# Weight loads in 8 KB runs per partition, with strided columns in the transposes and the gather that match them

## The chip, the core and the metric

The kernel runs on one core of one Trainium2 chip. TensorE (PE) multiplies, and loads its stationary operand with a separate instruction (PEld) that can overlap the product before it. VectorE (DVE), ScalarE (ACT) and GpSimd (POOL) do the element work, SyncE (SP) issues every transfer, and 16 DMA engines carry them out. The metric is the device time of one execution in microseconds, the median of three runs. A program without any change in it varies by about 1% from run to run here.

## The reference

Sequence length 256, model width 1024, float32. A first block of two layers is followed by a second block with a mixture of experts. Only two parts are touched, the feed-forward part of each layer and the experts:

```
# both layers of the first block; w_down has 2816 rows
gate, up = jnp.split(h @ ffn_w_gate_up, 2, axis=-1)
x = x + g_f * ((jax.nn.silu(gate) * up) @ ffn_w_down)
...
# second block: 16 experts, w_gate and w_up 1024 x 512, w_down 512 x 1024
for e in range(N_EXPERTS):
    h = jax.nn.silu(jnp.einsum("bsd,df->bsf", x, w_gate[e])) * jnp.einsum("bsd,df->bsf", x, w_up[e])
    y = y + combine[..., e:e + 1] * jnp.einsum("bsf,fd->bsd", h, w_down[e])
```

The router gives each token two experts out of one group of four, so that each expert has to be applied only to the tokens of its group.

## The kernel before

Every weight comes through a ring. A unit is 1 MB: 128 partitions of 2048 floats (`UNIT`). SP issues a unit's transfer as soon as a raw slot is free (`Ring.feed`, L159; it waits for DVE's `lo_done`). ACT then rounds the unit to a high part (`Ring.hi`, L172), DVE subtracts to get the low part (`Ring.lo`, L184), and each product on TensorE is done three times (high by high, high by low, low by high) on single-pass operands. The layers' ring (`layer_raw`, `layer_split`) has 4 raw slots and 3 pairs, the experts' ring (`expert_raw`, `expert_split`) has 5 and 4. The units' order is fixed when the program is built, and so is the order of each engine's work.

**Feed-forward part** (`FeedForward`, 11 blocks of 256 hidden columns in each of two layers). For a block, TensorE makes gate and up products (L459, 96 matmuls with 256 moving columns), the previous block's down product (L1894, 24 matmuls with 512 moving columns) and four transposes of the gated hidden values (L1882), whose results ACT and DVE split into `ffnh_aT` (L1929, L1962). The down weights of a block are one unit: 256 rows of 1024 floats. Partition p holds rows p and 128 + p of the block, so the transposes take hidden columns 0 to 127 and 128 to 255, each a run of neighbouring columns. In layer 0 the ring also brings the modulation weights `ada_w`, which DVE sums (L199 to L208).

**Experts** (`routed_experts`). After the routing, 16 pairs of gather matmuls (L2448, 32 in all) put the tokens of the four groups side by side: the stationary operand is a 128 x 128 piece of `x_pair`, columns 128c to 128c + 127, and the result is chunk c of the transposed tokens. Each expert then is 48 matmuls for gate and up (L2399, two units each), four transposes of the hidden values (L2410) and 24 matmuls for down (L2423, two units). In a gate or up unit partition p holds rows 128(k0 + k) + p for four k, so four runs of 512 floats; in a down unit two runs of 1024 floats.

In a transpose the stationary operand is the tile that is turned, and the moving one is the identity matrix, so the columns picked out by the slice in the code are the ones that the weight load reads.

Of the kernel before, what the change touches and what calls it, by code (L numbers as in the profile page):

```python
# [20 lines left out]
P = 128  # L21
D = 1024
S = 256
TILES = S // P
KD = D // P
# [7 lines left out]
D_EXPERT = 512  # L33
ALPHA = 2 ** 0.25
UNIT = 8 * 256
# [190 lines left out]
def program(nc, A, OUT):  # L226
    es = ExitStack()
    with es:
# [3 lines left out]
        ps = [es.enter_context(nc.psum_tensor(f"bank{b}", [P, 512], FP)) for b in range(8)]  # L232
# [14 lines left out]
        ident, ones = const("ident"), const("ones")  # L247
# [522 lines left out]
        def layers():  # L770
# [6 lines left out]
            def add(unit):  # L777
                units.append(unit)
                return len(units) - 1
# [21 lines left out]
            def layer_units(l, beside_proj, beside_gates, beside_ffn):  # L801
                w = {"proj": [], "gates": [], "branch": [], "out": []}
                p = pending_ada(beside_proj)
                w["proj"] = [None] * 8
                for i in (2, 3, 0, 1, 4, 5, 6, 7):
                    w["proj"][i] = add_cols("w_in", l, 256 * i, min(256 * i + 256, 1952))
                    ada_next(p)
                p = pending_ada(beside_gates)
                for b in range(12):
                    w["gates"].append(add_cols("w_in", l, 1952 + 256 * b, 2208 + 256 * b))  # L810
                    if b >= 7:
                        ada_next(p)
                for nb in range(2):
                    n0, n1 = 512 * nb, 512 * nb + 512

                    def part(name, row, k):
                        return (row * 512, k, 512, 0, 512, cols(name, l, n0, n1))

                    w["branch"].append((add([part("w_br_na", 0, 2), part("w_br_mla", 2, 2)]),
                                        add([part("w_br_gqa", 0, 4)])))  # L820
                for nb in range(4):
                    w["out"].append(add_cols("w_out", l, 256 * nb, 256 * nb + 256))
                p = pending_ada(beside_ffn)
                many = len(beside_ffn) > 1
                w["gu"], w["dn"] = [], []

                def down(n):
                    w["dn"].append(add([(0, 2, D, 0, D, A["ffn_w_down"][l, 256 * n:256 * n + 256, :]
                                         .rearrange("(k p) n -> p k n", p=P))]))
                    if many and n in (2, 4, 6, 8):  # L830
                        ada_next(p)

                for n in range(n_hidden):
                    pair = []
                    for up in range(2):
                        c0 = FFN * up + 256 * n
                        pair.append(add_cols("ffn_w_gate_up", l, c0, c0 + 256))
                        if many and n or (up and n in (1, 3, 5, 7)):
                            ada_next(p)
                    w["gu"].append(pair)  # L840
                    if n:
                        down(n - 1)
                down(n_hidden - 1)
                return w

            p = pending_ada([(0, 0), (0, 1)])
# [5 lines left out]
            with ExitStack() as st:  # L852
# [51 lines left out]
                for l in range(DEPTH):  # L904
                    LAYER[0] = f"_{l}"
                    w = where[l]
# [926 lines left out]
        class FeedForward:  # L1833
# [26 lines left out]
            def tensor(self, pe):  # L1860
                ring, ada, blocks, norm, gu, dn = self.ring, self.ada, self.blocks, self.norm, self.gu, self.dn

                def hidden(n, up, t):
                    ring.arrived(pe, gu(n, up))
                    if n >= 1 and t == 0:
                        pe.wait_ge(self.acted if up else self.multiplied, n)
                    job, out = Job(gu(n, up), "tok", t, 256, True, None), ps[up][:, t * 256:(t + 1) * 256]
                    if n:
                        ins = products(ring, job, out)
                    else:  # L1870
                        products(ring, job, out, pe, norm.ready(t), chunks=norm.ORDER[0:4], last=False)
                        if up and t == 0:
                            norm.turn(pe, 1)
                        ins = products(ring, job, out, pe, norm.ready(t), chunks=norm.ORDER[4:8], first=False)
                    if t == 1:
                        ins.then_inc(ring.used, 1)

                def turn(n):
                    pe.wait_ge(self.acted, n + 1)
                    for t in range(TILES):  # L1880
                        for c in range(2):
                            ins = nc.tensor.transpose(ps[2][:, c * S + t * P:c * S + (t + 1) * P],  # L1882
                                                      self.a[:, t, c * P:(c + 1) * P], ident)
                    ins.then_inc(self.turned, 1)

                def down(n):
                    pe.wait_ge(self.lo_out, n + 1)
                    ring.arrived(pe, dn(n))
                    for t in range(TILES):
                        for nb in range(2):  # L1890
                            for c in range(2):
                                for tp, wp in ((0, 0), (0, 1), (1, 0)):
                                    w = ring.view(dn(n), wp, 2, D)
                                    ins = nc.tensor.matmul(  # L1894
                                        ps[4 + 2 * t + nb][:, :], self.aT[:, tp, c, t * P:(t + 1) * P],
                                        w[:, c, nb * 512:(nb + 1) * 512],
                                        start=n == 0 and c + tp + wp == 0,
                                        stop=n == blocks - 1 and c == 1 and tp == 1)
                        if n == blocks - 1 and t == 0:
                            ins.then_inc(self.tile_sum, 1)  # L1900
                    ins.then_inc(ring.used, 1)

                for n in range(blocks):
                    for up, t in ((0, 0), (1, 0), (0, 1), (1, 1)) if n == 0 else ((0, 0), (0, 1), (1, 0), (1, 1)):
                        hidden(n, up, t)
                    if n and ada.due(gu(n, 0)):
                        ada.reduce(pe, 3, 1)
                        self.reduced_in[n] = 1
                    if n >= 1:
                        down(n - 1)  # L1910
                    turn(n)
                down(blocks - 1)
                self.ada_end = ada.done_pe
# [24 lines left out]
            def add(self, dve, t, half):  # L1938
                cut = slice(512 * half, 512 * half + 512)
                done(dve, nc.vector.tensor_tensor(self.buf.tmp[half], ps[4 + 2 * t + half][:, :], self.gate[:, cut], ALU.mult),  # L1940
                     self.step)
                done(dve, nc.vector.tensor_tensor(x[:, t, cut], x[:, t, cut], self.buf.tmp[half], ALU.add), self.added)
# [105 lines left out]
        def second_part():  # L2048
# [34 lines left out]
                return A[name][0, e, :, 256 * n:256 * n + 256].rearrange("(k p) n -> p k n", p=P)  # L2083

            expert_units, dense_units = [], []
            def rows_of(name, e, k0, k):
                return A[name][0, e, P * k0:P * (k0 + k), :].rearrange("(k p) n -> p k n", p=P)

            for e in range(N_EXPERTS + 1):
                if e < N_EXPERTS:  # L2090
                    for name in ("w_gate_2", "w_up_2"):
                        expert_units += [[(0, 4, 512, 0, 512, rows_of(name, e, k0, 4))] for k0 in (0, 4)]
                if e:
                    expert_units += [[(0, 2, D, 0, D, rows_of("w_down_2", e - 1, k0, 2))] for k0 in (0, 2)]
            n_hidden = N_EXPERTS * D_EXPERT // 256
            per = D_EXPERT // 256
            dense_units = hidden_units(n_hidden, lambda n: expert_half("w_gate_2", n // per, n % per),
# [20 lines left out]
            with ExitStack() as st:  # L2118
# [7 lines left out]
                with ExitStack() as s1:  # L2126
                    xP = sb("x3_pair", [P, 2, TILES, D], s1, FR)
# [220 lines left out]
        def routed_experts(ring, comb, xP, G, st, scratch, route, g_ready, combined):  # L2348
# [34 lines left out]
            with nc.Block() as block:  # L2383
# [9 lines left out]
                def _(pe):  # L2393
# [11 lines left out]
                    def turn(e):  # L2405
                        pe.wait_ge(acted, e + 1)
                        if e >= 1:
                            pe.wait_ge(a_lo, e)
                        for c in range(4):
                            ins = nc.tensor.transpose(ps[TURN][:, c * P:(c + 1) * P], act_[:, c * P:(c + 1) * P], ident)  # L2410
                        ins.then_inc(turned, 1)

                    def down(e):
# [29 lines left out]
                    for n in range(16):  # L2443
# [1 line left out]
                        if n >= 7:  # L2445
                            pe.wait_ge(*left(n - 7))
                        for t in range(TILES):
                            ins = nc.tensor.matmul(ps[PICK[n % 7]][:, :], xP[:, part, t, c * P:(c + 1) * P],  # L2448
                                                   G[:, t, :, :].rearrange("p g s -> p (g s)"), start=t == 0, stop=t == 1)
                        ins.then_inc(picked, 1)  # L2450
                        if n in TABLES:
# [1116 lines left out]
```

## Time and profile before

| | us |
|---|---|
| median of 3 runs | 1805.93 |
| lowest, highest run | 1790.78, 1807.78 |
| span of the profiled execution | 1795.4 |
| TensorE busy in it | 1597.9 (89%) |
| VectorE busy | 1225.5 (68%) |
| ScalarE busy | 817.2 (46%) |
| granted TensorE clock, mean share of full | 0.950 |

The span runs from the first to the last instruction of the profiled execution, which is another execution than the three timed ones. Matmuls are pipelined: the recorded time of one is longer than the distance from its start to the next one's. So a stretch of matmuls is best read by the starts of its groups.

### The profile page before, as it was taken

What the parts mean: (1) busy time and instruction counts of PE and PEld (TensorE: products, weight loads), DVE (VectorE), ACT (ScalarE), POOL (GpSimd) and SP (SyncE); (2) the same over time, 40 slices, a digit from 0 to 9 for tenths busy, and PEclk for the clock granted to TensorE, in tenths of its full rate; (3) what the DMA queues carried; (4) which work ended last, traced back from release to release, by engine and by line L of the source; (5) the groups of instructions that cost most, each with busy time, mean ns of one, the idle gap of its engine ahead of it and who ended that gap; (6) DMA issues with size and microseconds to landing.
All of it is one profiled execution on the core that took longest, in us unless ns stands there. A gap on an engine that the chain in (4) does not pass through costs nothing. (4 is left out here: it accounts for less than half of the span.)

```text
span 1795.4 us, 25499 instructions
## 1 busy us (share of the span) xinstructions
PE 1597.9 (89%) x10701; PEld 1443.7 (80%) x10701; DVE 1225.5 (68%) x1352; ACT 817.2 (46%) x945; POOL 43.9 (2%) x60
## 2 busy tenths in 40 slices
PE   2899998999899999899969998886788969999995
PEld 2789987999788988899959898775687767888884
DVE  4877586888757648656554885533565868889895
ACT  1345543433334554434323564224443337777773
POOL 0100000000010000000000000000000000000000
PEclk9989999999999999999989999987787989999998
DMA  8974435999844324566436463111231637999992
GB/s 306 316 236 141 163 121 172 351 331 325 276 139 145 110 94 164 182 215 230 137 110 197 147 188 118 47 48 31 64 118 34 203 138 262 370 343 369 357 357 100
DMA packets 226057, 348.07 MB, mean 194 GB/s; under 512 B 14612, under 2 KB 156672, under 8 KB 225808
## 3 DMA queue, kind: packets, MB, share of 16 engines
q1 hardware_dynamic: 225936, 346.36, 57.7%
q8 instruction: 87, 1.43, 0.3%
q14 instruction: 34, 0.28, 0.0%
HBM read 345.29 MB, written 1.97 MB: 193 GB/s over the span
## 5 line engine op out<-in xcount | busy, mean ns | idle before, releaser
L459 PE MATMUL bank<-layer_split,hT_pair 128*128 128x256 f32 (+2 forms) x4032 | 514.3, 288 | 29.7 <-DVE hT_pair L1031 21.0
L459 PEld LDWEIGHTS bank<-layer_split,hT_pair 128*128 128x128 f32 x4032 | 488.0, 191 | 43.6 <-issue 28.9
L184 DVE TENSOR_TENSOR layer_split<-layer_raw,layer_split 128x2048 fp32r<-128x2048 f32 x122 | 279.6, 2292 | 101.6 <-ACT layer_split L172 99.9
L172 ACT ACTIVATE layer_split<-layer_raw 128x2048 fp32r<-128x2048 f32 x122 | 233.6, 1915 | 192.0 <-PE bank L459 76.9
L184 DVE TENSOR_TENSOR expert_split<-expert_raw,expert_split 128x2048 fp32r<-128x2048 f32 x96 | 219.1, 2289 | 30.4 <-ACT expert_split L172 30.2
L172 ACT ACTIVATE expert_split<-expert_raw 128x2048 fp32r<-128x2048 f32 x96 | 183.6, 1917 | 59.0 <-PE bank L2399 32.8
L459 PE MATMUL bank<-split_w,hT_pair 128*128 128x256 f32 (+1 forms) x1248 | 173.2, 301 | 14.9 <-PEq L2600 5.0
L459 PEld LDWEIGHTS bank<-split_w,hT_pair 128*128 128x128 f32 x1248 | 163.1, 201 | 25.7 <-issue 17.1
L184 DVE TENSOR_TENSOR split_w<-raw_w,split_w 128x2048 fp32r<-128x2048 f32 x52 | 119.2, 2292 | 64.2 <-ACT split_w L172 63.6
L1894 PE MATMUL bank<-layer_split,ffnh_aT 128*128 128x512 f32 x528 | 127.0, 396 | 2.8 <-DVE ffnh_aT L1962 2.8
L172 ACT ACTIVATE split_w<-raw_w 128x2048 fp32r<-128x2048 f32 x52 | 99.4, 1912 | 58.9 <-PE bank L459 50.1
L459 PE MATMUL bank<-hT_pair,split_w 128*128 128x256 f32 x960 | 119.5, 285 | 5.5 <-DVE hT_pair L315 4.8
L459 PEld LDWEIGHTS bank<-hT_pair,split_w 128*128 128x128 f32 x960 | 116.9, 192 | 7.4 <-issue 5.7
L1894 PEld LDWEIGHTS bank<-layer_split,ffnh_aT 128*128 128x128 f32 x528 | 98.0, 188 | 25.8 <-DVE ffnh_aT L1962 3.3
L2423 PE MATMUL bank<-expert_split,expert_hidden_T 128*128 128x512 f32 x384 | 92.3, 396 | 1.4 <-DVE expert_hidden_T L2563 1.4
L2399 PE MATMUL bank<-expert_split,hT_pair 128*128 128x512 f32 x384 | 92.5, 397 | 0.9 <-ACT gathered_pair L2492 0.9
L2399 PE MATMUL bank<-expert_split,gathered_pair 128*128 128x512 f32 x384 | 90.8, 392 | 0.0
L2423 PEld LDWEIGHTS bank<-expert_split,expert_hidden_T 128*128 128x128 f32 x384 | 72.1, 188 | 18.9 <-DVE expert_hidden_T L2563 1.6
L2399 PEld LDWEIGHTS bank<-expert_split,hT_pair 128*128 128x128 f32 x384 | 71.5, 188 | 18.0 <-ACT gathered_pair L2492 1.3
L2399 PEld LDWEIGHTS bank<-expert_split,gathered_pair 128*128 128x128 f32 x384 | 71.5, 188 | 14.9
L204 DVE SCALAR_TENSOR_TENSOR ada_acc<-layer_raw,silu_c,ada_acc 128x1024 f32<-128x1024 f32 x40 | 51.7, 1294 | 1.4
L1929 ACT ACTIVATE ffnh_aT<-bank 128x512 fp32r<-128x512 f32 x22 | 13.1, 597 | 80.0 <-PE bank L1882 80.0
(459 smaller groups left out, 1795.1 us busy)
## 6 DMA issues: line engine op xcount, KB each, us to landing
layer_raw<-in_ada_w SPq DMA_DIRECT2D x48, 1024.0 KB, 6.7
layer_raw<-in_ffn_w_gate_up SPq DMA_DIRECT2D x44, 1024.0 KB, 5.6
raw_w<-in_w_in SPq DMA_DIRECT2D x40, 1024.0 KB, 5.4
layer_raw<-in_w_in SPq DMA_DIRECT2D x38, 1024.0 KB, 5.9
expert_raw<-in_w_gate SPq DMA_DIRECT2D x32, 1024.0 KB, 7.5
expert_raw<-in_w_up SPq DMA_DIRECT2D x32, 1024.0 KB, 7.4
expert_raw<-in_w_down SPq DMA_DIRECT2D x32, 1024.0 KB, 7.1
layer_raw<-in_ffn_w_down SPq DMA_DIRECT2D x22, 1024.0 KB, 5.1
```

The source lines that it names most:

```text
L172: self.nc.scalar.activation(self.pair[:, j % self.pairs, 0, 0:self.size[n]], self.raw[:, n % self.depth, 0:self.size[n]], ACT.Copy).then_i ...
L184: self.nc.vector.tensor_tensor(self.pair[:, j % self.pairs, 1, 0:self.size[n]], self.raw[:, n % self.depth, 0:self.size[n]], self.pair[:, ...
L204: self.nc.vector.scalar_tensor_tensor(acc[:, :], second, self.scale[:, 2 * q + 1:2 * q + 2], acc[:, :], ALU.mult, ALU.add).then_inc(self.l ...
L459: ins = nc.tensor.matmul(out, lhs, rhs, start=first and c == chunks[0] and tp + wp == 0, stop=last and c == chunks[-1] and tp == 1)
L1894: ins = nc.tensor.matmul(ps[4 + 2 * t + nb][:, :], self.aT[:, tp, c, t * P:(t + 1) * P], w[:, c, nb * 512:(nb + 1) * 512], start=n == 0 an ...
L1929: nc.scalar.activation(self.aT[:, 0, :, :].rearrange(flat), ps[2][:, :], ACT.Copy).then_inc(self.hi_out, 1)
L2399: ins = nc.tensor.matmul(ps[bank][:, :], gathered[e // PER // 2][:, tp, 4 * i + c, slot_cut(e // PER)], ring.view(u + i, wp, 4, 512)[:, c, :],
L2423: ins = nc.tensor.matmul(ps[OUT_BANKS[nb]][:, :], aT[:, tp, 2 * i + c, :], ring.view(u + i, wp, 2, D)[:, c, nb * 512:(nb + 1) * 512], star ...
```

## The change

The same weights go into the same units in the same order, but in each unit a partition now holds neighbouring rows of the matrix. A gate or up matrix of an expert is read as 128 partitions of 8 neighbouring rows, 16 KB each, and the two units are the first and the second 8 KB of each partition; a down matrix is 128 partitions of 4 neighbouring rows, again 16 KB in two halves; a block of `ffn_w_down` is 128 partitions of 2 neighbouring rows, 8 KB. The transfer's source is then one run of 2048 floats for each partition.

The contraction index that sits on partition p, chunk k, becomes K p + k rather than 128 k + p, with K = 2, 8 and 4. To match, the feed-forward transposes take every second column, the gather takes every eighth column of `x_pair`, and the experts' transposes take every fourth column of the hidden values. The products themselves, and the number and the order of the instructions on every engine, stay as they were.

```
--- before.py
+++ after.py
                 def down(n):
-                    w["dn"].append(add([(0, 2, D, 0, D, A["ffn_w_down"][l, 256 * n:256 * n + 256, :]
-                                         .rearrange("(k p) n -> p k n", p=P))]))
+                    w["dn"].append(add([(0, 1, UNIT, 0, UNIT, A["ffn_w_down"][l, 256 * n:256 * n + 256, :]
+                                         .rearrange("(p k) n -> p (k n)", p=P).unsqueeze(1))]))
...
                             ins = nc.tensor.transpose(ps[2][:, c * S + t * P:c * S + (t + 1) * P],
-                                                      self.a[:, t, c * P:(c + 1) * P], ident)
+                                                      self.a[:, t, c:256:2], ident)
...
-            def rows_of(name, e, k0, k):
-                return A[name][0, e, P * k0:P * (k0 + k), :].rearrange("(k p) n -> p k n", p=P)
+            def run_of(name, e, i):
+
+                return A[name][0, e, :, :].rearrange("(p k) n -> p (k n)", p=P)[:, UNIT * i:UNIT * (i + 1)].unsqueeze(1)
...
-                        expert_units += [[(0, 4, 512, 0, 512, rows_of(name, e, k0, 4))] for k0 in (0, 4)]
+                        expert_units += [[(0, 1, UNIT, 0, UNIT, run_of(name, e, i))] for i in range(2)]
                 if e:
-                    expert_units += [[(0, 2, D, 0, D, rows_of("w_down_2", e - 1, k0, 2))] for k0 in (0, 2)]
+                    expert_units += [[(0, 1, UNIT, 0, UNIT, run_of("w_down_2", e - 1, i))] for i in range(2)]
...
-                            ins = nc.tensor.transpose(ps[TURN][:, c * P:(c + 1) * P], act_[:, c * P:(c + 1) * P], ident)
+                            ins = nc.tensor.transpose(ps[TURN][:, c * P:(c + 1) * P], act_[:, c:D_EXPERT:4], ident)
...
-                            ins = nc.tensor.matmul(ps[PICK[n % 7]][:, :], xP[:, part, t, c * P:(c + 1) * P],
+                            ins = nc.tensor.matmul(ps[PICK[n % 7]][:, :], xP[:, part, t, c:D:KD],
                                                    G[:, t, :, :].rearrange("p g s -> p (g s)"), start=t == 0, stop=t == 1)
```

## Rows read from the trace of the kernel before

**Rows 1.** The page: busy time, DMA packets by size, DMA queues.

```profile
PE 1597.9 (89%) x10701; PEld 1443.7 (80%) x10701; DVE 1225.5 (68%) x1352; ACT 817.2 (46%) x945; POOL 43.9 (2%) x60
...
DMA packets 226057, 348.07 MB, mean 194 GB/s; under 512 B 14612, under 2 KB 156672, under 8 KB 225808
...
q8 instruction: 87, 1.43, 0.3%
q14 instruction: 34, 0.28, 0.0%
```

**Rows 2.** Busy time by stretch: feed-forward of layer 0, of layer 1, experts.

```profile
core 0: us, PE busy (x) PEld busy (x) DVE busy (x) ACT busy (x) POOL busy (x), PEclk, DMA share, GB/s
320.00:480.00 160.00, 160.00 (x1173) 148.84 (x1172) 137.33 (x108) 63.08 (x46) 0.00 (x0) 1.00 0.96 330
740.00:900.00 160.00, 160.00 (x1180) 149.88 (x1179) 93.03 (x66) 62.44 (x47) 0.00 (x0) 1.00 0.59 197
1500.00:1760.00 260.00, 260.00 (x1157) 211.58 (x1156) 230.37 (x138) 189.67 (x126) 0.00 (x0) 1.00 0.99 355
```

**Rows 3.** Waits from 320 to 480 us: total us, times, longest.

```profile
ACT layer_split L172 <- DMA layer_raw<-in_ffn_w_gate_up: 36.3, 10, 5.7
...
ACT layer_split L172 <- DMA layer_raw<-in_ffn_w_down: 7.8, 5, 2.7
```

**Rows 4.** Timeline of PE, one expert: start, us, group of matmuls.

```profile
1510.15 5.85 PE L2399 MATMUL bank<-expert_split,hT_pair 128*128 128x512 f32 x24
1515.84 5.76 PE L2423 MATMUL bank<-expert_split,expert_hidden_T 128*128 128x512 f32 x24
1521.43 5.76 PE L2399 MATMUL bank<-expert_split,hT_pair 128*128 128x512 f32 x24
1527.03 0.60 PE L2410 MATMUL bank<-cst,silu_hidden 128*128 128x128 f32 x4
1527.38 2.81 PE L2399 MATMUL bank<-expert_split,hT_pair 128*128 128x512 f32 x11
```

**Rows 5.** Waits from 1500 to 1760 us, of ACT and of SP's queue.

```profile
ACT expert_split L172 <- PE bank L2399: 30.0, 42, 1.3
...
SPq L159 <- DVE expert_split L184: 220.3, 87, 4.3
```

**Rows 6.** DMA queue q1 and issues with time to landing: 1500 to 1760, then 740 to 900.

```profile
q1 hardware_dynamic: 38234, 92.12, 98.3%
...
expert_raw<-in_w_gate SPq DMA_DIRECT2D x28, 1024.0 KB, 7.6
```

```profile
q1 hardware_dynamic: 21051, 31.29, 58.6%
...
layer_raw<-in_ffn_w_down SPq DMA_DIRECT2D x10, 1024.0 KB, 5.0
```

**Rows 7.** Timeline of PE: down product under full DMA, and with none.

```profile
332.24 5.63 PE L1894 MATMUL bank<-layer_split,ffnh_aT 128*128 128x512 f32 x24
337.71 0.60 PE L1882 MATMUL bank<-cst,na_qkT 128*128 128x128 f32 x4
```

```profile
903.36 5.63 PE L1894 MATMUL bank<-layer_split,ffnh_aT 128*128 128x512 f32 x24
908.83 0.60 PE L1882 MATMUL bank<-cst,na_qkT 128*128 128x128 f32 x4
```

**Rows 8.** Weight loads of the three lines that change: ns min/median/max.

```profile
L1882 PEld LDWEIGHTS bank<-cst,na_qkT x88: 138/141/230, 301.6 to 909.0; 128*128 128x128 f32 x88
```

```profile
L2410 PEld LDWEIGHTS bank<-cst,silu_hidden x64: 137/140/143, 1509.6 to 1766.4; 128*128 128x128 f32 x64
```

```profile
L2448 PEld LDWEIGHTS bank<-gather_table,x_pair x32: 187/192/333, 1479.3 to 1491.4; 128*128 128x128 f32 x32
```

**Rows 9.** The page: both splits of an expert unit: busy us, mean ns, idle before.

```profile
L184 DVE TENSOR_TENSOR expert_split<-expert_raw,expert_split 128x2048 fp32r<-128x2048 f32 x96 | 219.1, 2289 | 30.4 <-ACT expert_split L172 30.2
...
L172 ACT ACTIVATE expert_split<-expert_raw 128x2048 fp32r<-128x2048 f32 x96 | 183.6, 1917 | 59.0 <-PE bank L2399 32.8
```

## The prediction

> **What bounds the kernel now.** I first read the page: TensorE is busy for 1597.9 us (89% of the span), DVE for 1225.5, ACT for 817.2 [rows 1]. So TensorE is the engine to ask, but the page is a mean over stages, and the change touches three: the feed-forward parts, the gather, and the experts. The busy time by stretch shows TensorE at 160.00 of 160 us in the body of the feed-forward part of layer 0, at 160.00 of 160 in that of layer 1, and at 260.00 of 260 in the experts, at the full granted clock in all three [rows 2]. The DMA engines are at 0.96, 0.59 and 0.99 in the same stretches. A reader may take the 0.96 and 0.99 for a bound, and then a more efficient transfer would be worth a lot. Four views speak against that.
>
> First, the two layers are a comparison that the kernel makes by itself. Both run the same blocks, layer 0 with the modulation weights beside them, at 330 GB/s, layer 1 at 197 GB/s. TensorE gets through 1173 matmuls in 160 us in the one and 1180 in the other [rows 2]. Seven matmuls, at 160 / 1180 = 0.136 us each, are 1 us: all that a crowded DMA can cost TensorE there, and layer 0 also has reductions of its own in that stretch.
>
> Second, in layer 0 weights do land late, but for ACT: it waits 36.3 us for gate and up units and 7.8 us for down units [rows 3]. These waits end in slack between ACT, DVE and TensorE, since TensorE has no gap in the same stretch [rows 2].
>
> Third, in the experts nobody waits for a transfer at all: ACT waits for TensorE to free a pair (42 times, 30.0 us, for the gate and up products alone), and SP waits 220.3 us for DVE to free a raw slot [rows 5]. The transfers run at the pace at which slots come free. An expert takes TensorE 17.23 us for its 6 units, by the starts of its pieces: 1515.84 - 1510.15 = 5.69 us for 24 up products, 1521.43 - 1515.84 = 5.59 us for the down products, 1527.03 - 1521.43 = 5.60 us for the gate products and 1527.38 - 1527.03 = 0.35 us for the four transposes [rows 4]. That is 2.87 us for a unit of 1.05 MB, or 365 GB/s.
>
> Fourth, DMA traffic does not slow the products either. The 24 down products of a feed-forward block take 337.71 - 332.24 = 5.47 us with the DMA at 0.96, and 908.83 - 903.36 = 5.47 us at the end of layer 1, when all weights have landed [rows 7].
>
> **The transfers, part by part.** Removed: 64 gate and up units of 4 x 128 runs of 2 KB (32768 runs), 32 down units of the experts and 22 of the feed-forward part of 2 x 128 runs of 4 KB (13824 runs; 46592 together). Added: 118 units of 128 runs of 8 KB, 15104 runs. A long run travels as one packet: packets of 8 KB or more are 226057 - 225808 = 249 now, which is the 87 + 34 of the instruction queues and 128 rows of the second block's table of constants [rows 1]. So I expect about 194600 packets, of which 179200 under 8 KB, and 156672 under 2 KB as before.
>
> What a byte costs the DMA engines: experts, 0.983 x 16 x 260 / 92.12 = 44.4 engine-us per MB at 38234 / 92.12 = 415 packets per MB; layer 1, 0.586 x 16 x 160 / 31.29 = 47.9 at 673 per MB [rows 6]. From the two, a packet costs 3.5 / 258 = 0.014 us and a MB without packets 38.8. With 8 KB runs (122 per MB) a MB costs 40.5 engine-us: an estimate, since the two stretches differ in more than packets. At an unchanged 355 GB/s [rows 2] the share of the DMA falls from 0.99 to about 0.355 x 40.5 / 16 = 0.90. A gate unit that now lands 7.6 us after its issue should land nearer the 5.0 of layer 1 [rows 6], where less is in flight. Worth on the path: nothing in the experts and in layer 1, at most the 1 us above in layer 0. The cover is TensorE's own work. If TensorE were somehow 10% faster, the transfers would be next in line; here nothing makes it faster. The transfers that are issued behind these units (SP's queue is one line) move up by the same microseconds, and none of them is waited for by TensorE while it is busy.
>
> **The strided columns.** These are on the path, since TensorE is. Touched are the weight loads of 88 feed-forward transposes (a step of 8 bytes), 64 expert transposes (16 bytes) and 32 gather matmuls (32 bytes); medians now are 141, 140 and 192 ns [rows 8]. No load of the trace has a step, so I bound. Below: no change, 0 us. A gain is excluded, as a load with a step reads no less than one without. Above: each load takes twice as long and nothing hides it, 152 x 0.14 = 21.3 us and 32 x 0.19 = 6.1 us, 27 us together. Which end is nearer? Four transposes go by in 0.35 us although their loads take 4 x 0.14 = 0.56 us [rows 4, 8]: part of a load already lies under the work before it. A load of 128 columns in 140 ns is 1.1 ns per column, slow beside the 0.23 us in which a product takes in 512 moving columns [rows 4]; so the load seems to be paced by something else than the fetching of neighbouring bytes. The gather's load of 192 ns [rows 8] lies under a product of 512 columns, and those start 5.59 / 24 = 0.23 us apart [rows 4]. I take 0, and keep 27 for the range.
>
> A rule speaks against the change here. The Trainium skill (SBUF — State Buffer, Door 1: The DMA port swizzle, and Advanced Engine Details and Errata, SBUF Cachelines) says that the memory is read in lines of 16 bytes, that an access needs at least two hits on a line for full speed, and that a step that lands on a new line each time pays a penalty. By it the feed-forward transposes (two hits) stay free, and the experts' transposes and the gather pay. No row here shows a step of that size on TensorE, so the trace can't say whether it agrees.
>
> **The sum.** -1 to 0 us from the transfers, 0 from the loads: the time of before. The profiled execution had a span of 1795.4 us, 10.5 below the median of the three runs and 4.6 above the lowest (1790.78), so four executions of one program fall around 1791, 1795, 1806 and 1808. A middle of these is nearer 1801 than 1806. With the change worth nothing I predict 1803 us, between that middle and the median of 1805.93. About 1%, 18 us, is what a measurement here can tell from no change.
>
> **Rivals.**
> 1. *Loads with steps of 16 bytes or more slow down.* For: nothing in the trace excludes it, and TensorE has no slack in the experts. Against: the cover above. Price: 64 x 0.14 + 6.1 = 15 us, hence 1818 us, still within 1% of 1805.93. Chance 0.10. This is the rule of the pages quoted.
> 2. *All loads with a step slow down, the 8 bytes too.* Price 27 us, hence 1830 us, slower. It decides once a group of four transposes takes more than about 0.35 + 0.4 us. Chance 0.05.
> 3. *The new pattern in HBM is slower.* Before, an expert unit was 1 MB in one piece; now it is every other 8 KB, with 16 KB from partition to partition. Only the experts would feel it. The DMA has little spare: a unit may take 2.87 us at most. Landing may grow by some 3 us before ACT feels it (five slots are 5 x 2.87 = 14.4 us, less 1.9 + 2.3 us for the two splits [rows 9], less 7.6 for the landing). For: the share is at 0.99 already. Against: fewer packets. At 10% longer transfers the 276 us of the experts grow by up to 10%, 27 us, hence 1830 us, slower. Chance 0.04.
> 4. *The DMA was a hidden bound and the kernel gets faster.* The 24 products take 5.59 to 5.69 us in the experts and 5.47 in the feed-forward part [rows 4, 7]. If that came from the DMA writing beside them, 48 groups x 0.17 = 8 us could be had, and with all of ACT's 7.8 us [rows 3] on the path 16 us: 1787 us. Against: 5.47 us with the DMA full and empty. Chance 0.06; over 1% only with a low set of runs.
> 5. *The change doesn't do what it says:* 8 KB runs are cut into smaller packets again. Then the packet count stays near 226000, and the time stays as well, so it shares the forecast's number. It shows in the page, not in the time.
>
> **How the numbers follow.** No change of the time: 0.75, its own range 1789 to 1810, which is the spread of the four executions. Rivals 1 to 4: 0.25. For the range, the low end is 1788, just under the lowest run; the high end is 1823, which takes in rival 1 with its spread and leaves out rivals 2 and 3 and most of the gain of rival 4. Faster by over 1% (below 1788): rival 4 and a low set of runs, 0.08. Slower by over 1% (above 1824): rivals 2 and 3, and a third of rival 1 with a high set of runs, 0.12. Within 1%: 0.80.
>
> **What the profile of the changed kernel would show.** Packets at 194600 (179200 under 8 KB). The share of the DMA in the experts near 0.90 with the same GB/s, and landing below 7 us. ACT's waits for transfers in layer 0 shorter. Medians of the weight loads at L1882, L2411 and L2449 (the lines move by one) unchanged at 141, 140 and 192 ns, the distance over four transposes 0.35 us, an expert every 17.2 us. TensorE busy through the three stretches. The forecast is wrong if the loads' medians or the 17.2 us move, or if ACT waits for `expert_raw` transfers; and on the other side, if TensorE gets through visibly more matmuls per 20 us than now.

## The result, and the profile after

The changed kernel takes 1806.51 us, the median of 20 runs (1801.04 to 1813.13). The kernel before, run 20 times as well, takes 1798.60 us (1790.78 to 1807.78). The medians lie 7.9 us apart. The ratio is 1.0047, with a 95% interval from 1.0034 to 1.0060: by it the change costs 8.5 us, at least 6.1 and at most 10.8. That lies inside the 1% that the prediction called no change, and 1806.51 lies inside its range, but the loss is clear of the noise and the forecast had none.

The first three runs of before (1790.78, 1805.93, 1807.78) had two high ones among them: their median stood 7 us above the median of 20.

The page of the changed kernel, busy time and packets:

```profile
span 1809.3 us, 25499 instructions
...
PE 1614.7 (89%) x10701; PEld 1463.4 (81%) x10701; DVE 1226.8 (68%) x1352; ACT 817.8 (45%) x945; POOL 44.1 (2%) x60
...
DMA packets 194569, 348.07 MB, mean 192 GB/s; under 512 B 14612, under 2 KB 156672, under 8 KB 179216
```

Beside [rows 1]: the packets fell from 226057 to 194569, as worked out. DVE and ACT have the busy time they had. What grew is TensorE, by 16.8 us of recorded matmul time, and its weight loads, by 19.7 us.

The weight loads of the three lines that changed (ns, min/median/max; L2411 and L2449 are L2410 and L2448 of before), to be read against [rows 8]:

```profile
L1882 PEld LDWEIGHTS bank<-cst,na_qkT x88: 194/207/222, 303.1 to 915.7; 128*128 128x128 f32 x88
```

```profile
L2411 PEld LDWEIGHTS bank<-cst,silu_hidden x64: 197/205/212, 1521.7 to 1779.2; 128*128 128x128 f32 x64
```

```profile
L2449 PEld LDWEIGHTS bank<-gather_table,x_pair x32: 313/333/345, 1490.9 to 1503.6; 128*128 128x128 f32 x32
```

A transpose's load went from 140 to about 206 ns, whether its step is 8 bytes (L1882) or 16 (L2411); the gather's went from a median of 192 to 333. On the path that is little. The timeline of TensorE for one expert (start, us, group):

```profile
1533.64 5.77 PE L2400 MATMUL bank<-expert_split,hT_pair 128*128 128x512 f32 x24
1539.25 0.63 PE L2411 MATMUL bank<-cst,silu_hidden 128*128 128x128 f32 x4
1539.64 5.84 PE L2400 MATMUL bank<-expert_split,hT_pair 128*128 128x512 f32 x24
```

The four transposes take 1539.64 - 1539.25 = 0.39 us from start to start where they took 0.35 [rows 4]: 16 experts x 0.04 = 0.6 us. The whole expert part, from the first expert product to the last, grew by just that, from 280.8 to 281.4 us. The 22 feed-forward blocks give at most 22 x 0.04 = 0.9 us more, and the gather went from 13.64 us, first product to first expert product, to 1505.09 - 1490.93 = 14.16 us, 0.5 us. Together 2.0 us of 7.9 to 8.5. Where is the rest?

It is in the feed-forward parts, at a line that the change does not touch. TensorE's timeline in layer 1, after:

```profile
777.30 0.63 PE L1882 MATMUL bank<-cst,na_qkT 128*128 128x128 f32 x4
777.68 11.14 PE L459 MATMUL bank<-layer_split,hT_pair 128*128 128x256 f32 x96
788.66 5.64 PE L1894 MATMUL bank<-layer_split,ffnh_aT 128*128 128x512 f32 x24
794.14 0.63 PE L1882 MATMUL bank<-cst,na_qkT 128*128 128x128 f32 x4
794.53 11.55 PE L459 MATMUL bank<-layer_split,hT_pair 128*128 128x256 f32 x96
805.92 5.63 PE L1894 MATMUL bank<-layer_split,ffnh_aT 128*128 128x512 f32 x24
811.40 0.63 PE L1882 MATMUL bank<-cst,na_qkT 128*128 128x128 f32 x4
811.78 11.14 PE L459 MATMUL bank<-layer_split,hT_pair 128*128 128x256 f32 x96
```

and before:

```profile
789.76 11.14 PE L459 MATMUL bank<-layer_split,hT_pair 128*128 128x256 f32 x96
...
806.57 11.14 PE L459 MATMUL bank<-layer_split,hT_pair 128*128 128x256 f32 x96
```

The same 96 gate and up products take 11.14 us in one block and 11.55 us in the next. From start to start the products are 113 to 114 ns apart in the one and 118 in the other, and the pace that the first five or so settle into holds for all 96. I call the second the slow pace; it costs 0.41 us a block. There are 20 blocks (of 22) whose 96 products follow straight behind the four transposes. Read off the timeline for all of them, before has 1 slow block of 20, after has 10, nearly every second one: 9 more, 3.7 us. With the 2.0 us that makes 5.7 us of the 7.9 to 8.5.

The transfers, after (1520 to 1760 us: queue share of 16 engines, issues with the time to landing), and before in the same stretch:

```profile
q1 hardware_dynamic: 11843, 86.18, 97.1%
...
expert_raw<-in_w_gate SPq DMA_DIRECT2D x26, 1024.0 KB, 6.6
```

```profile
q1 hardware_dynamic: 35421, 85.19, 98.4%
...
expert_raw<-in_w_gate SPq DMA_DIRECT2D x26, 1024.0 KB, 7.6
```

A third of the packets carry the same bytes, and a unit lands 1.0 us sooner. In the experts nobody was waiting for it.

### The profile page after: what moved, and what is told of

Its sections match the earlier page's. It is cut to its first block and busy times, and to the rows that moved or that the text cites. A ratio compares the mean times of both kernels' runs of the same rounds, so it can differ in the third digit from the quotient of the medians.

```text
span 1809.3 us, 25499 instructions
## 1 busy us (share of the span) xinstructions
PE 1614.7 (89%) x10701; PEld 1463.4 (81%) x10701; DVE 1226.8 (68%) x1352; ACT 817.8 (45%) x945; POOL 44.1 (2%) x60
## 2 busy tenths in 40 slices
DMA packets 194569, 348.07 MB, mean 192 GB/s; under 512 B 14612, under 2 KB 156672, under 8 KB 179216
## 5 line engine op out<-in xcount | busy, mean ns | idle before, releaser
L459 PE MATMUL bank<-layer_split,hT_pair 128*128 128x256 f32 (+2 forms) x4032 | 520.7, 290 | 29.9 <-DVE hT_pair L1031 21.1
L459 PEld LDWEIGHTS bank<-layer_split,hT_pair 128*128 128x128 f32 x4032 | 494.8, 192 | 43.5 <-issue 29.0
L459 PE MATMUL bank<-split_w,hT_pair 128*128 128x256 f32 (+1 forms) x1248 | 178.7, 307 | 13.5 <-PEq L2601 5.0
L459 PEld LDWEIGHTS bank<-split_w,hT_pair 128*128 128x128 f32 x1248 | 168.8, 206 | 23.9 <-issue 16.3
L1894 PE MATMUL bank<-layer_split,ffnh_aT 128*128 128x512 f32 x528 | 127.0, 396 | 2.8 <-DVE ffnh_aT L1962 2.8
L1894 PEld LDWEIGHTS bank<-layer_split,ffnh_aT 128*128 128x128 f32 x528 | 98.0, 188 | 25.7 <-DVE ffnh_aT L1962 3.2
L2400 PEld LDWEIGHTS bank<-expert_split,gathered_pair 128*128 128x128 f32 x384 | 71.6, 188 | 14.9
```

Source lines behind the costliest of these rows:

```text
L459: ins = nc.tensor.matmul(out, lhs, rhs, start=first and c == chunks[0] and tp + wp == 0, stop=last and c == chunks[-1] and tp == 1)
L1894: ins = nc.tensor.matmul(ps[4 + 2 * t + nb][:, :], self.aT[:, tp, c, t * P:(t + 1) * P], w[:, c, nb * 512:(nb + 1) * 512], start=n == 0 an ...
L2400: ins = nc.tensor.matmul(ps[bank][:, :], gathered[e // PER // 2][:, tp, 4 * i + c, slot_cut(e // PER)], ring.view(u + i, wp, 4, 512)[:, c, :],
```

## The experiments

The ratios are to the kernel before, timed beside each on the same chip, and a loss in us is worked out from the ratio. Edits are against before.

**e1: only the strided columns.**

```
-  self.a[:, t, c * P:(c + 1) * P], ident)
+  self.a[:, t, c:256:2], ident)
...
-  act_[:, c * P:(c + 1) * P], ident)
+  act_[:, c:D_EXPERT:4], ident)
...
-  xP[:, part, t, c * P:(c + 1) * P],
+  xP[:, part, t, c:D:KD],
```

> The weights are loaded as before, and only the columns are strided (feed-forward transposes by 2, expert transposes by 4, gather by 8); the contraction rows no longer match, so the output is another one, the work is the same. Theory A (the strided weight loads on TensorE cost everything): the whole loss of the change, about 8 us or 0.4 to 0.5% over the kernel before; weight loads of the transposes near 205 ns and of the gather at full clock near 328 ns, about half of the feed-forward blocks with gate and up products 118 ns apart rather than 113 to 114. Rival B (the 8 KB transfers cost it, by their pattern in HBM or on the way into SBUF): no difference to before, within 2 us. Rival C (the loss has no place, the kernels differ by luck of the clock): within 2 us as well, with long loads but the same pace of the products.

Measured: 1.0029 (1.0016 to 1.0042), 5.2 us. Loads of 207 ns at L1882, 9 of 20 blocks slow. The sum for it is 8 x 0.41 + 2.0 = 5.3 us; the 8 us that I expected were more than that. Rivals B and C are out as accounts of the whole: with the transfers of before, about two thirds of the loss is there, and the interval does not reach down to no loss.

**e2: only the 8 KB transfers** (`ffn_w_down` and the experts' units as in the change, columns as before).

> Only the 8 KB transfers, with the columns of the transposes and the gather left as runs of neighbours; the rows no longer match, so the output is another one, the work is the same. Theory A: within 2 us of before (0.1%), DMA share in the experts lower as in the changed kernel (about 0.95), weight loads at 140 ns. Rival B: about 8 us slower. A gain of more than 2 us would mean that the transfers do give something that the strided loads take back.

Measured: 1.0003 (0.9984 to 1.0022), that is, from 2.9 us faster to 4.0 slower; 1 of 20 blocks slow. The transfers neither cost nor give anything that can be measured.

**e3: only the feed-forward part**, transfers and transposes by 2.

> Only the feed-forward part is changed, its down weights and its transposes by 2. Theory A splits the loss by the two traces: the two feed-forward parts are 2.7 + 2.0 = 4.7 us longer in the changed kernel, so 4 to 5 us slower than before, of which only 22 x 0.03 = 0.7 us is the transposes themselves and the rest the slower pace of the products behind them in every second block. If steps of 8 bytes cost nothing but the transposes' own time, it would be under 1 us.

Measured: 1.0029 (1.0013 to 1.0045), 5.2 us; 9 of 20 blocks slow, in the same alternation.

**e4: only the experts and the gather.**

> Only the experts' weights, their transposes by 4 and the gather by 8 are changed. Theory A by the traces: gather 0.5 us and experts 0.6 us longer, 1.1 us in all, and every feed-forward block as in the kernel before. More than 3 us would mean that a share of the loss comes from places that the change does not touch (routing, mixer).

Measured: 1.0007 (0.9990 to 1.0023), 1.3 us; 1 of 20 blocks slow. Most of the loss sits in the feed-forward part, as its share of the sum said, and e3 and e4 together give 1.0036.

The loads of the down products (L1894) in layer 1 mark the length of that part, from the first start to the last: 166.2 us before, 168.1 after, and in e3, e2:

```profile
L1894 PEld LDWEIGHTS bank<-layer_split,ffnh_aT x264: 186/188/192, 750.8 to 918.6; 128*128 128x128 f32 x132
```

```profile
L1894 PEld LDWEIGHTS bank<-layer_split,ffnh_aT x264: 186/188/189, 747.8 to 913.6; 128*128 128x128 f32 x132
```

167.8 us with strided transposes and 165.8 without, whatever the transfers are: e1, which has the transfers of before, gives 167.8 us as well.

**e5: the kernel before once more.**

> The kernel before once more, for a second profile of it. If the pace of the feed-forward products is set by the program (theory A), at most 2 of the 20 blocks that open with 96 gate and up products right behind the transposes are slow (118 ns from product to product), as in the first profile, and the two feed-forward parts and the experts last what they lasted, within 0.5 us where the clock is the same. If the pace is luck (rival C), the count can be anything.

Measured: 0 of 20 blocks slow. The part in layer 1 lasted 0.4 us less than in the first profile, as one slow block less asks for.

**e6: the changed kernel once more.**

> The changed kernel once more, timed beside the others. Theory A: about every second feed-forward block slow again (8 to 12 of 20), gather 0.5 us and experts 0.6 us longer than before, ratio to before 1.003 to 1.006. Of the loss of 8 us, the pieces that have a place give 5.8 us; if the rest is real, some other stage must show a longer time again in this profile, and if it is luck, that stage's time is as before.

Measured: 1.0043 (1.0025 to 1.0062); 11 of 20 blocks slow, alternating as before. In these 20 blocks the count comes from the program: 1 and 0 in two profiles of before, 10 and 11 in two of the changed kernel.

Outside these blocks the pace varies between profiles of one program. Two long stretches of products with 256 moving columns, which the change does not touch, show it. In the first profile of before:

```profile
939.40 43.37 PE L459 MATMUL bank<-hT_pair,split_w 128*128 128x256 f32 x366 [0.30 <-DVE hT_pair L315]
...
1433.70 22.02 PE L459 MATMUL bank<-split_w,hT_pair 128*128 128x256 f32 x192 [0.85 <-DVE hT_pair L315]
```

and in the second, e5:

```profile
936.49 41.76 PE L459 MATMUL bank<-hT_pair,split_w 128*128 128x256 f32 x366 [0.23 <-DVE hT_pair L315]
...
1431.01 22.85 PE L459 MATMUL bank<-split_w,hT_pair 128*128 128x256 f32 x192 [0.85 <-DVE hT_pair L315]
```

The first stretch is slow in one profile and fast in the other (1.6 us), the second the other way round (0.8 us). In both profiles of the changed kernel both are slow, 1.2 us more than the mean of the two of before.

The granted clock differs too. Over the 32 runs of the changed kernel (the 20 of the result and the 12 of e6) its mean is 0.948, over the 87 runs of before timed beside the experiments 0.950 (on the chip of e6 alone, 12 runs against 23, the two means are 0.948 and 0.950 as well); the difference is 0.0019, with a 95% interval from about 0.0010 to 0.0027. What such a difference is worth can be read from the routing, from its first transposes to the gather, in the two profiles of before (the number behind POOL is the granted clock):

```profile
1464.40:1479.30 14.90, 9.82 (x59) 9.34 (x59) 11.56 (x31) 10.13 (x10) 0.33 (x1) 0.61 0.69 253
```

```profile
1462.50:1480.30 17.80, 12.71 (x59) 12.30 (x59) 11.66 (x31) 10.13 (x10) 0.36 (x1) 0.50 0.58 213
```

In both the clock fell from its full level, 2.4 GHz, to half, 1.2 GHz, during the 8.65 us in which TensorE waited for DVE ahead of this stretch. At full clock for part of the stretch (mean 0.61) it takes 14.9 us, at half the clock throughout 17.8 us: 2 x 0.39 x 14.9 = 11.6 us at half the clock in the one, 17.8 in the other, so 6.2 us more at half the clock cost 2.9 us. A difference of 0.0019 over 1800 us is 2 x 0.0019 x 1800 = 6.8 us more at half the clock, which at that price is an estimated 3 us. Both profiles of the changed kernel have the long routing.

So the 2 to 3 us between the sum and the measured loss have two candidates, the pace in other stretches and the clock. No run shows that the change brings either about, and this part of the cause stays open. The interval of e6 reaches down to the sum of 5.7 us (1.0025 is 4.5 us); that of the result, from 6.1 us on, does not.

**e7: the 8 KB transfers, with the columns put in order when the tiles are written.**

```
-  nc.vector.tensor_tensor(self.a.rearrange(flat), ps[1][:, :], g, ALU.mult)
+  nc.vector.tensor_tensor(self.a.rearrange("p t (c q) -> p t c q", c=2),
+                          ps[1][:, :].rearrange("p (t q c) -> p t c q", t=TILES, c=2),
+                          g.rearrange("p (t q c) -> p t c q", t=TILES, c=2), ALU.mult)
```

and in the same way `act_` with 4 and both parts of `x_pair` with 8.

> The 8 KB transfers are kept, and the columns are put in the order that matches them when the tiles are written: DVE reads the gated hidden values (steps 2 and 4) and ACT and DVE read x for its pair (step 8) with a step and write runs, so that every transpose and gather loads neighbouring columns. The output is the reference's. Theory A: loads back at 140 and 188 to 192 ns, at most 2 slow feed-forward blocks of 20, gather and experts as before, and the time of the kernel before within 0.1%, if the strided reads on DVE and ACT take no longer than now; if they take twice as long, 22 + 16 instructions of 0.7 us lie on a chain with slack and four splits of 1 us lie on the path of the routing, 2 to 4 us. Rival B (the transfers cost it): about 8 us slower as the changed kernel.

Measured: 1.0012 (0.9997 to 1.0027); 1 of 20 blocks slow. The strided reads do cost, on the other engines: ACT's write of `x_pair`, e7 and then before (ns, min/median/max):

```profile
L2280 ACT ACTIVATE x_pair<-x x2: 2042/2068/2093, 1464.9 to 1466.9; 128x1024 fp32r<-128x1024 f32 x2
```

```profile
L2277 ACT ACTIVATE x_pair<-x x2: 1045/1047/1049, 1468.1 to 1469.1; 128x1024 fp32r<-128x1024 f32 x2
```

and DVE's product of an expert's hidden values (busy us, mean ns), 745 ns before:

```profile
L2579 DVE SCALAR_TENSOR_TENSOR silu_hidden<-bank,slot_weights,silu_hidden 128x512 f32<-128x512 f32 x16 | 18.0, 1126 | 0.0
```

So this version repairs the change but does not beat the kernel before; none that I ran does.

**e8: the changed kernel with the last feed-forward transpose done twice.**

```
                     for t in range(TILES):
                         for c in range(2):
                             ins = nc.tensor.transpose(ps[2][:, ...], self.a[:, t, c:256:2], ident)
+                    ins = nc.tensor.transpose(ps[2][:, ...], self.a[:, t, c:256:2], ident)
                     ins.then_inc(self.turned, 1)
```

> The changed kernel with the last transpose of each feed-forward block done twice (same operands and place, so the output stays the reference's). By its own time it costs 22 x 0.12 = 2.6 us. If the slow pace of the products is a matter of the strided load itself, the same every second block is slow and the kernel is 2.6 us slower than the changed one. If it is a matter of the moment at which the products begin against some slower beat (theory A in its narrower form), one more transpose shifts that moment, and the count of slow blocks changes, to anywhere from none (1.5 us faster than the changed kernel) to all (6.7 us slower).

Measured: 1.0070 (1.0050 to 1.0091), 9 of 20 blocks slow. The changed kernel, timed beside it, is e6 with 1.0043: this one is 4.9 us slower, where the transposes' own time is 2.6 us, and the two intervals overlap. By itself this spoke for the strided load as the cause and against the moment: the shift of 120 ns left the alternation as it was.

**e9: the kernel before with the last transpose done twice.**

> The kernel before with the last transpose of each feed-forward block done twice, and no strided load anywhere; the output stays the reference's. By its own time it costs 22 x 0.11 = 2.4 us. If the slow pace of the products needs a strided load, at most 2 of 20 blocks are slow and the kernel is 2.4 us (0.13%) slower than before. If it depends only on the moment at which the products begin, the count of slow blocks moves with the shift, and each one adds 0.41 us, up to 8 us more.

Measured: 1.0022 (0.9999 to 1.0045), 4.0 us where the transposes' own time is 2.4 us and lies inside the interval; no slow block in 20. Plain loads keep the fast pace here as well.

**e10: three strided transposes, the last one plain; e11: the mirror.** Both have the 8 KB down weights in the feed-forward part and the experts of before. Each was run once, for its profile (1809.49 and 1807.36 us, too few runs to compare times).

```
e10:  self.a[:, t, c * P:(c + 1) * P] if t and c else self.a[:, t, c:256:2], ident)
e11:  self.a[:, t, c:256:2] if t and c else self.a[:, t, c * P:(c + 1) * P], ident)
```

> 8 KB down weights in the feed-forward part; of its four transposes the first three load with a step of 2 and the last one neighbouring columns (so the output is another one, the work is the same); experts as before. If the last load, which is the one right ahead of the products, sets their pace, no more than 2 of 20 blocks are slow and the gap to the first product is 28 to 29 ns again in place of 40. If the moment at which they begin does, the count can be anything, and need not be what a plain or a strided set gives.

> The mirror: the first three transposes load neighbouring columns and the last one with a step of 2 (the output is another one, the work is the same); experts as before. If the last load sets the pace of the products, about every second block is slow (8 to 12 of 20), as in the changed kernel, and the gap to the first product is 40 ns. If it is the moment, the count can be anything.

Measured: e10 has 19 of 20 blocks slow, e11 10 of 20. TensorE's timeline in e10:

```profile
778.27 0.62 PE L1882 MATMUL bank<-cst,na_qkT 128*128 128x128 f32 x4
778.65 11.55 PE L459 MATMUL bank<-layer_split,hT_pair 128*128 128x256 f32 x96
...
795.90 11.55 PE L459 MATMUL bank<-layer_split,hT_pair 128*128 128x256 f32 x96
...
813.14 11.55 PE L459 MATMUL bank<-layer_split,hT_pair 128*128 128x256 f32 x96
```

and in e11:

```profile
777.33 11.14 PE L459 MATMUL bank<-layer_split,hT_pair 128*128 128x256 f32 x96
...
794.15 11.55 PE L459 MATMUL bank<-layer_split,hT_pair 128*128 128x256 f32 x96
...
811.37 11.14 PE L459 MATMUL bank<-layer_split,hT_pair 128*128 128x256 f32 x96
```

The last load is not what sets the pace: with a plain one right ahead of the products nearly all blocks are slow, and with a single strided one half of them are. Nor is it the number of strided loads: four give half, three give nearly all, one gives half. What is left, by elimination, is how the sequence of loads comes out in time against the products, which repeats from block to block. One reading fits it: in both profiles of the changed kernel the four transposes ahead of a slow block take 348 or 349 ns from the first start to the last, and those ahead of a fast one 345 or 346 (the first block of each layer left out). So the two patterns differ before the first product starts. No run names the mechanism any closer.

**e12: e10, timed.**

> The kernel of e10 once more (three strided transposes and a plain last one in the feed-forward part, experts as before, output another one, work the same), now timed. In its profile 19 of the 20 blocks were slow, where the kernel before has 0 or 1 and the feed-forward change with four strided transposes 9. If the pace of the products is what the change costs, this kernel is slower than before by 19 x 0.41 = 7.8 us and 22 x 0.02 = 0.5 us for the transposes, 0.4 to 0.5%, more than e3 (0.29%), although it has fewer strided loads. If the strided loads themselves are what costs, it is three quarters of e3's, 0.2% slower.

Measured: 1.0045 (1.0027 to 1.0062), 8.1 us; 19 of 20 blocks slow again. The sum was 8.3 us. With fewer strided loads than e3 it does not lose less, so the pace is what is paid for, not the loads: 19 slow blocks at 0.41 us carry 7.8 of the 8.1 us. The interval of e3 reaches up to 1.0045, so the times alone do not put the two in order. The feed-forward part of layer 1 does:

```profile
L1894 PEld LDWEIGHTS bank<-layer_split,ffnh_aT x264: 186/188/192, 754.1 to 923.8; 128*128 128x128 f32 x132
```

It lasts 169.7 us, where e3 has 167.8 and a part without slow blocks (e2) 165.8.

## Why the prediction was right and wrong

**TensorE as the bound: right.** It stayed without a gap in the experts, and every microsecond lost that has a place is one of its.

**The transfers, worth nothing: right, and tested.** e2 gives 1.0003 (0.9984 to 1.0022). The packet counts came out as worked out. ACT's waits in layer 0 fell (28.1 us for gate and up units where [rows 3] has 36.3) and bought nothing. The sized estimate behind it was off: I took a packet's price from two stretches and expected the share of the DMA in the experts at 0.90. It is 0.97. By the bytes, 0.971 x 16 x 240 / 86.18 = 43.3 engine-us per MB against 44.4 before and 40.5 expected. The two stretches differ in crowding as well as in packets, and so can't price a packet. Probably the share also counts time in which a packet only waits; no run separates the two.

**The strided loads, worth nothing: the step that failed.** I bounded them by 0 and 27 us and took 0, on the argument that a load of 140 ns is slow beside what a product reads and so is not paced by fetching neighbours. The step does lengthen them: 140 to 206 ns, and 188 to 328 ns for the gather at the full clock. The term was 0 in the sum and is 2.0 us on the path, without the products behind the loads. The second half of the argument, that most of this lies under the work around it, held: 152 loads grew by 66 ns, 10 us, of which 1.5 us reached the path, and 32 by up to 140 ns, 4.5 us, of which 0.5 did.

**What the prediction did not have** is the larger term. It priced an instruction by itself and took the 96 products behind it as fixed. They are not: they have two paces, and in the feed-forward blocks the count of slow ones changes with the loads of the four transposes ahead of them (e1, e2, e10). 9 to 11 slow blocks more make 3.7 to 4.5 us, about half of the loss. The profile of before had both paces to show: one block of 20 is slow, at 755 us, and so are the 366 products from 939 us on.

**The rivals.** Rival 1 (steps of 16 bytes or more cost, 8 bytes do not) has the direction, but its 15 us are 1.1 us, and its dividing line is wrong. The trace agrees with the rule of the Trainium skill that I quoted for it (Advanced Engine Details and Errata, SBUF Cachelines) only in that steps of 16 and 32 bytes cost: the transposes with a step of 8 bytes, with two hits on a line, slow down as much (141 to 207 ns) as those of 16 bytes with one (140 to 205 ns). A larger step of 32 bytes, in the gather, does cost more; its operand is of another kind, so that the step alone can't be blamed. Rival 2 (all steps cost) named the right set of instructions and put 27 us on it; its threshold, 0.75 us for four transposes, was far off the 0.39 us that came. Rivals 3 and 4 are refuted by e2, and rival 5 by the count of packets.

**The number.** With before at 1798.6, no change would have been 1799. I started 4 us above that because of the three runs that I had. That part of 1803 was luck of the right sign.

## What to carry to other kernels

When a kernel is bound by TensorE, a layout that helps the transfers is paid for at the operand that has to match it: put the step where an idle engine reads it, or nowhere, and count on 0 from transfers that nobody waits for. Do not price an edit in a dense stream of matmuls by its own instructions alone; read the spacing of the untouched ones behind it, before and after, since a pace once taken is kept over a hundred products. And a difference of half a per cent is read from undisturbed stages and repeated profiles, not from the span: here one stage (the routing, at half the granted clock for a varying part of it) took 14.9 and 17.8 us in two profiles of one program.

## What the runs showed of the hardware

- Products of 256 moving columns, each with its own weight load, run 113 to 114 ns or 118 ns apart at the full granted clock, and keep the one they settle into for 96 products and for 366. The count of slow feed-forward blocks came out at 1 and 0 of 20 in two profiles of one program, 10 and 11 in two of the other, 19 and 19 in two of a third. In other stretches the pace changed between two profiles of one program (366 products in 43.37 and in 41.76 us). Products of 512 columns behind the experts' transposes show no difference between before and after (5.59 to 5.69 us for 24 in both).
- A step in the stationary operand makes the load longer, by the same amount for 8 and 16 bytes (141 to 207 ns and 140 to 205). At half the granted clock (0.50 from 1479 to 1484 us before, 0.52 from 1490 to 1496 us after) it does not: the gather's first loads take 330 ns without a step and 334 with one. Before, from 1479 us on, and after, from 1490 us on:

```profile
L2448 PEld LDWEIGHTS bank<-gather_table,x_pair x14: 188/330/333, 1479.3 to 1484.5; 128*128 128x128 f32 x14
```

```profile
L2449 PEld LDWEIGHTS bank<-gather_table,x_pair x14: 316/334/338, 1490.9 to 1496.0; 128*128 128x128 f32 x14
```

The later ones, at the full clock, before and after:

```profile
L2448 PEld LDWEIGHTS bank<-gather_table,x_pair x18: 187/188/192, 1485.5 to 1491.4; 128*128 128x128 f32 x18
```

```profile
L2449 PEld LDWEIGHTS bank<-gather_table,x_pair x18: 313/328/345, 1497.1 to 1503.6; 128*128 128x128 f32 x18
```

- ACT reads a tile with a step of 32 bytes at half its speed (1.05 to 2.07 us), and DVE took 1126 ns in place of 745 for one product that read both its bank and its tile with a step of 16 bytes. With a step of 8 bytes DVE's product in the feed-forward part took 689 ns in e7, as before: that step costs on TensorE's loads and not there.
